# The last output pair and the next stage's first chunks of a ten-stage transformer kernel, worked off in two halves of the tokens

## Chip, cores and metric

One core of a Trainium2 chip. The metric is the device time of one execution in microseconds, lower is better; times are medians of several executions.

## What is computed

Three transformer layers over 512 tokens of width 1024, in float32. The first has a mixer of dilated attention, a state-space scan and a gated recurrence, then a SwiGLU feed-forward; the two that follow have a feed-forward, a mixer (block-sparse attention with compressed keys beside a retention), an attention over 256 memory tokens and a second feed-forward. Around every stage stands a root-mean-square norm:

```python
def rms_norm(x, g):
    xf = x.astype(jnp.float32)
    y = xf * lax.rsqrt(jnp.mean(xf * xf, axis=-1, keepdims=True) + EPS)
    return (y * g.astype(jnp.float32)).astype(x.dtype)
...
x = x + 0.5 * rms_norm(swiglu(rms_norm(x, pre_g), ...), post_g)
```

The mixer and the memory attention have the factor 1 in place of 0.5. Where two stages meet, the output y of one needs its own norm before it is added to x, and the new x needs another one before it is the input of the next.

## The kernel before, in words

**Layout.** x lies in SBUF with the features on the 128 partitions and 512 tokens along the columns, as 8 tiles of 128x512. Each float32 product is three matmuls (`mm3`, lines 255 to 257): operands are kept as a high part (rounded to the matmul's format) and a low part, and high x high, low x high and high x low are added in PSUM. Weights come as chunks of 8 tiles x 256 columns, in two DMAs of 512 KB (halves) on SyncE's queue. ScalarE makes the high part of a half (`weight_hi`, line 235), GpSimd the low part (`weight_lo`, line 249). Four slots hold halves; a slot is free when the chunk two before has been used.

**Engines.** Each engine has a program written out by hand, stage after stage, and works in that order; semaphores tie them. TensorE's order is the one given here.

**The end of a stage** (`OutProj`, `OutSums`). The output has 8 tiles in four pairs. A pair is 22 (feed-forward) or 8 (mixer, attention) tiles deep, in chunks of at most 8; each chunk runs its first output tile over all depths, then its second (`pe_stationary`). After a pair, ScalarE copies the tile out of PSUM (line 508) and squares it (line 511), VectorE adds the squares (line 497). Sums over the partitions are matmuls against a column of 1/1024 (`pe_token_means`, line 355): those of the first seven tiles run before the last product, those of the eighth after it. In the first block's feed-forward (`onto`) VectorE adds the product to x first (line 491).

**Between stages** (`Entry`). The means get epsilon on VectorE (line 542), the power -1/2 on GpSimd (line 547), and TensorE spreads the roots over the partitions (line 555) into a row bank; `pe_keep_busy` (line 562) stands before and after. VectorE meanwhile makes the low parts of the second chunk's weights. Then, tile by tile: y times gain and root (line 609; with kind "final" x itself, line 612, and no add), x plus y (line 619), the high part of x times the next gain on ScalarE (line 672), the low part on VectorE (line 624). VectorE issues them in the order scale of the next tile, low, add of the next tile. The input is not divided by its own root; results of the first products are multiplied with that row later. ScalarE squares the new x (line 661), four tiles beside the high parts, four after them; VectorE adds the squares (line 648) after its last tile.

**The start of a stage** (`pe_by_tile`, line 317 on). The first two chunks run together, tile by tile, as soon as a tile's low part is there. Then `pe_then` (line 716 on) waits for the last sum of squares, makes the means of x (line 355), and goes on with the third chunk; the row of roots follows after a few products.

**Start and end.** At the start ScalarE squares x (line 377), GpSimd adds the squares (line 389), TensorE sums them (line 346), and GpSimd makes the power (line 417) behind four low parts of weights; x comes in four DMAs, the constants (1.1 MB) between the first and the second. At the end (`Exit`) VectorE scales and adds (lines 746 and 750) and one DMA stores 2 MB. In the retention VectorE sums and centres each head's output (lines 2549 and 2555), ScalarE squares it with an accumulator (line 2519).

## Time and profile before

| what | value |
|---|---|
| time, median of 3 (lowest, highest) | 3376.74 us (3374.31, 3379.72) |
| the profiled execution's own time | 3378.53 us |
| its span, first to last instruction | 3377.2 us |
| mean granted TensorE clock | 0.987 |
| TensorE busy | 97% |
| VectorE, ScalarE, GpSimd busy | 38%, 36%, 39% |
| DMA, mean over the span | 85 GB/s |

Busy shares are means over the span. TensorE's busy time counts a matmul from its issue to its modelled end, so that overlapping ones hide short gaps; the spacing of their starts tells more. PEclk is the share of full speed (2.4 GHz) that was granted: 1.0, or 0.5 (1.2 GHz). A row of the timeline has start, duration, engine, line, operation, output<-inputs, count, and in brackets the idle time before it with what ended it. PE is TensorE, PEld its weight loads, DVE VectorE, ACT ScalarE, POOL GpSimd, SP SyncE. A plain float32 matmul (lines 346, 355, 555) appears as two instructions, so 4 of them are counted as x8.

### The profile page before, as it was taken

The numbers are of one execution on the slowest core, as the hardware profiler recorded it, in microseconds if no ns is written. First come the engines' busy times: TensorE is split into PE (matmuls) and PEld (weight loads), VectorE is DVE, ScalarE is ACT, GpSimd is POOL, SyncE is SP. The second block draws the span as 40 slices with busy tenths as digits, with TensorE's granted clock in tenths as the row PEclk, the third lists the DMA queues.
The fourth block names the chain that finished last, engine by engine and source line by source line (L and its number), as shares of the span: only waits on it lengthen the run. The fifth ranks groups of instructions, "written<-read, shape, count | busy, mean of one in ns | idle before, by whom it ended". The sixth has DMA issues, their size and how long they took to land.

```text
span 3377.2 us, 42103 instructions
## 1 busy us (share of the span) xinstructions
PE 3261.2 (97%) x16304; PEld 2676.1 (79%) x16304; DVE 1299.0 (38%) x2343; ACT 1219.4 (36%) x2237; POOL 1307.8 (39%) x831
## 2 busy tenths in 40 slices
PE   5999999999999999999999999999999999999997
PEld 4886788887888788887678887888787887678886
DVE  4564343205330434644263304431144563353311
ACT  4454332223222344553332223322344554332221
POOL 3452344443444343343234443444342243234442
PEclk9998999999999999999999999999999999999999
DMA  3221132232322232122122232332241122123231
GB/s 127 77 74 50 57 101 93 95 105 75 100 97 95 81 128 63 51 82 81 50 81 94 97 103 75 100 100 94 94 138 51 44 83 75 50 75 106 94 101 61
DMA packets 79109, 287.08 MB, mean 85 GB/s; under 512 B 8896, under 2 KB 9152, under 8 KB 78400
## 3 DMA queue, kind: packets, MB, share of 16 engines
q1 hardware_dynamic: 77616, 278.42, 25.1%
q10 hardware_dynamic: 1296, 5.98, 0.5%
q8 instruction: 131, 2.15, 0.3%
q14 instruction: 66, 0.54, 0.0%
HBM read 282.26 MB, written 2.10 MB: 84 GB/s over the span
## 4 chain that ended last, share of the span: by engine, by line
PE 83%; DVE 6%; POOL 3%; ACT 3%; issue 3%; DMA 1%; ACTq 0%; POOLq 0%; DVEq 0%
PE bank L255 25%; PE bank L257 24%; PE bank L256 24%; PE bank L965 3%; POOL wlo L249 2%; PE bank L941 2%; PE bank L952 2%; DVE hlo L624 1%; ACT hhi L672 1%; DVE x L619 1%; ACT whi L235 1%; PE bank L2684 1%; PE bank L555 1%; DVE m_xbc L1558 1%; POOL stat L547 1%
## 5 line engine op out<-in xcount | busy, mean ns | idle before, releaser
L249 POOL TENSOR_TENSOR wlo<-raw,whi 128x1024 fp32r<-128x1024 f32 (+2 forms) x782 | 1260.7, 1627 | 1881.0 <-ACT whi L235 1846.8
L255 PE MATMUL bank<-hhi,whi 128*128 128x512 f32 x2416 | 964.7, 399 | 19.0 <-POOL wlo L249 10.8
L256 PE MATMUL bank<-hlo,whi 128*128 128x512 f32 x2456 | 958.6, 390 | 0.0
L257 PE MATMUL bank<-hhi,wlo 128*128 128x512 f32 x2416 | 944.2, 391 | 0.0
L235 ACT ACTIVATE whi<-raw 128x1024 fp32r<-128x1024 f32 (+1 forms) x536 | 534.8, 1034 | 384.7 <-PE bank L257 374.1
L255 PEld LDWEIGHTS bank<-hhi,whi 128*128 128x128 f32 x2416 | 455.4, 188 | 125.0 <-issue 30.0
L256 PEld LDWEIGHTS bank<-hlo,whi 128*128 128x128 f32 x2456 | 463.3, 189 | 91.3 <-issue 1.2
L257 PEld LDWEIGHTS bank<-hhi,wlo 128*128 128x128 f32 x2416 | 454.8, 188 | 96.9
L255 PE MATMUL bank<-ff_ahi,whi 128*128 128x512 f32 x880 | 342.8, 390 | 0.0
L257 PE MATMUL bank<-ff_ahi,wlo 128*128 128x512 f32 x880 | 342.4, 389 | 0.0
L256 PE MATMUL bank<-ff_alo,whi 128*128 128x512 f32 x840 | 326.8, 389 | 0.0
L497 DVE TENSOR_TENSOR tmp<-tmp,tmp 128x512 f32<-128x512 f32 x60 | 48.0, 800 | 562.3 <-ACT tmp L511 562.3
L850 ACT ACTIVATE ff_ahi<-tmp 128x512 fp32r<-128x512 f32 x110 | 69.6, 633 | 444.6 <-DVE tmp L873 444.6
L863 DVE TENSOR_TENSOR tmp<-bank,row 128x512 f32<-128x512 f32 x110 | 75.0, 690 | 366.5 <-PE bank L257 319.0
L980 ACT ACTIVATE att_s<-att_s,stat 128x32 f32<-128x32 f32 (+4 forms) x224 | 110.0, 491 | 275.5 <-DVE stat L1012 274.5
L257 PEld LDWEIGHTS bank<-ff_ahi,wlo 128*128 128x128 f32 x880 | 165.2, 188 | 34.3
L255 PEld LDWEIGHTS bank<-ff_ahi,whi 128*128 128x128 f32 x880 | 165.2, 188 | 34.1
L256 PEld LDWEIGHTS bank<-ff_alo,whi 128*128 128x128 f32 x840 | 157.7, 188 | 32.7
L844 ACT ACTIVATE tmp<-tmp 128x512 f32<-128x512 f32 x110 | 68.7, 630 | 308.4 <-DVE tmp L863 308.4
L871 DVE TENSOR_TENSOR tmp<-bank,row 128x512 f32<-128x512 f32 x110 | 75.8, 689 | 223.9 <-PE bank L257 223.9
L255 PE MATMUL bank<-whi,hhi 128*128 128x256 f32 x448 | 134.5, 300 | 0.1
L1008 DVE SCALAR_TENSOR_TENSOR att_s<-consts,bank 128x32 f32<-128x32 f32 (+4 forms) x192 | 72.9, 380 | 158.1 <-PE bank L941 157.7
(343 smaller groups left out, 4165.8 us busy)
## 6 DMA issues: line engine op xcount, KB each, us to landing
raw<-wstream SPq DMA_DIRECT2D x516, 512.0 KB, 3.7
raw<-wstream SPq DMA_DIRECT2D x20, 256.0 KB, 3.0
x<-xT ACTq DMA_DIRECT2D x4, 512.0 KB, 12.9
xa_v<-memT ACTq DMA_DIRECT2D x2, 1024.0 KB, 4.7
outT<-x SPq DMA_DIRECT2D x1, 2048.0 KB, 6.2
consts<-consts ACTq DMA_DIRECT2D x1, 1135.0 KB, 9.5
m_lw<-lru_w ACTq DMA_DIRECT2D x1, 544.0 KB, 3.5
par<-par SPq DMA_DIRECT2D x2, 248.0 KB, 14.1
```

What stands on the lines that cost most here:

```text
L235: a.activation(h.hi[:, 0:h.cols], h.raw[:, 0:h.cols], ACT.Copy).then_inc(h.hi_made.sem)
L249: last = g.tensor_tensor(h.lo[:, o:o + step], h.raw[:, o:o + step], h.hi[:, o:o + step].bitcast(F32), ALU.subtract)
L255: t.matmul(out, l[0], r[0], start=start, stop=False)
L256: t.matmul(out, l[0], r[1], start=False, stop=False)
L257: return t.matmul(out, l[1], r[0], start=False, stop=stop)
L844: a.activation(k.tmp[2 + m][:, :], k.tmp[m][:, :], ACT.Tanh, scale=0.5).then_inc(self.tanh.sem)
L850: a.activation(self.ahi[:, o:o + T], k.tmp[m][:, :], ACT.Copy).then_inc(self.hi_made.sem)
L863: v.tensor_tensor(k.tmp[m][:, :], k.bank[gate.banks[m]][:, :], k.row[:, :], ALU.mult).then_inc(self.normed.sem)
L871: v.tensor_tensor(k.tmp[m][:, :], k.bank[up.banks[m]][:, :], k.row[:, :], ALU.mult).then_inc(self.up.sem)
L965: last = t.matmul(k.bank[b][:, at:at + DH], p[0:rows, kb * P:(kb + 1) * P], u["v"](kb), start=kb == 0, stop=kb == nb - 1, skip_group_check ...
L980: a.activation(s[:, 0:n], s[:, 0:n], ACT.Exp, bias=k.stat[:, 80 + step % 4:81 + step % 4], accum_out=self.sums(g)[0][:, step % group:step ...
L1008: v.scalar_tensor_tensor(s[:, 0:n], u["dist"], u["slope"], k.bank[b][:, 0:n], ALU.mult, ALU.add).then_inc(self.biased.sem)
```

## The change

Eight boundaries and the exit go by halves of 256 tokens. A stage's last pair keeps half 0 of both output tiles in one bank and half 1 in the other: its earlier chunks run both halves product by product (`pe_both`), the last chunk all of half 0 and then all of half 1 (`pe_halves`), with half 0's sums, roots and row placed between half 1's products. Squares and copies of the two tiles are one ScalarE instruction a half. The input is made in 16 half tiles, half 0 first, and the next stage's first two chunks run once a half (`pe_by_tile_halves`); half 1's sums and row stand after tiles 0 and 2 of half 0. So each of these products is two matmuls of 256 columns, with the weights loaded twice. The second chunk's first half of weights lies in memory of the stage that ends (`spare`), and GpSimd makes its low part; the other half's low part moves from VectorE to GpSimd, in four pieces. `pe_keep_busy` goes. The boundary from the first mixer to its feed-forward stays as it was, as a class of its own. Further: at the start TensorE sums the squares tile by tile, the low part of the fourth half comes after the power, and most of the constants load last; the exit scales by halves and stores in four DMAs; the retention takes its sums from ScalarE's accumulator, centres within the square and the gating, and gates with one instruction a chunk.

```diff
+def mm3_half(k, out, l, r, half, opens):
+    t, r = k.nc.tensor, [x[:, half * TH:(half + 1) * TH] for x in r]
+    t.matmul(out, l[0], r[0], start=opens, stop=True, skip_group_check=True)
+    t.matmul(out, l[0], r[1], start=False, stop=True, skip_group_check=True)
+    return t.matmul(out, l[1], r[0], start=False, stop=True, skip_group_check=True)
...
+def pe_by_tile_halves(k, chunks, part, ready, then):
+    t = k.nc.tensor
+    for half in range(2):
+        for i in range(KT + len(chunks) - 1):
+            for lag, ch in enumerate(chunks):
+                kk = i - lag
+                if not 0 <= kk < KT:
+                    continue
+                if half == 0:
+                    pe_half_begin(k, ch, kk)
+                if lag == 0:
+                    for mark in ready(kk, half):
+                        t.wait_ge(*mark)
+                for m, b in enumerate(ch.banks):
+                    if half == 0 and kk == 0 and ch.free[m] is not None:
+                        t.wait_ge(*ch.free[m])
+                    last = mm3_half(k, k.bank[b][:, half * TH:(half + 1) * TH], ch.weights(kk, m * P, P), part(kk), half,
+                                    half == 0 and kk == 0)
+                    if half == 1:
+                        pe_step_end(ch, last, kk, kk == KT - 1, m == len(ch.banks) - 1)
+            then(half, i)
...
-        t.wait_ge(*self.added[-1])
-        if self.free is not None:
-            t.wait_ge(*self.free)
-        pe_token_sums(self.k, self.k.tmp[2][:, :], 0, True).then_inc(self.sums.sem)
+        for n in range(KT):
+            t.wait_ge(*self.sq[n])
+            pe_token_sums(self.k, self.tile(n)[:, :], 0, n == 0).then_inc(self.summed.sem)
...
+    def act_squares(self, half):
+        a, k = self.k.nc.scalar, self.k
+        a.wait_ge(*self.added[2 + half])
+        a.wait_ge(*(self.kept[6 + half] if self.onto else self.last.done[half]))
+        src = self.half_of(k.x, half) if self.onto else self.both(self.in_bank(half))
+        a.activation(self.both(self.squares(half)), src, ACT.Square).then_inc(self.sq.sem)
+    def act_keep(self, half):
+        a, k = self.k.nc.scalar, self.k
+        if not self.onto:
+            a.activation(self.half_of(self.y, half), self.both(self.in_bank(half)), ACT.Copy).then_inc(self.kept.sem)
...
+    def pe_six(self, half):
+        t = self.k.nc.tensor
+        if half == 0:
+            t.wait_ge(*self.added[-1])
+            if self.free is not None:
+                t.wait_ge(*self.free)
+        else:
+            t.wait_ge(*self.roots[0].mean[0])
+        self.pe_add(self.k.tmp[2], half * TH, half, half == 0)
+    def pe_two(self, half):
+        self.k.nc.tensor.wait_ge(*self.sq[6 + half])
+        self.pe_add(self.squares(half), 0, half, False)
+        self.pe_add(self.squares(half), TH, half, False).then_inc(self.mean.sem)
...
+        k.elsewhere[self.first + 1] = stage.spare()
...
+        self.before = sums.roots = [HalfRoot(k, sums, half, (row_bank, sums.b)[half]) for half in range(2)]
...
     def dve(self):
         k, v = self.k, self.k.nc.vector
-        if self.kind == "plain":
-            for n in range(KT):
-                self.low(n)
-        else:
-            self.before.dve()
-            weight_lo(k, self.first + 1, e=v)
-            v.wait_ge(*self.before.rows[0])
-            self.scale(0)
-            self.add(0)
+        self.before[0].dve()
+        for half in range(2):
+            v.wait_ge(*self.before[half].rows[0])
+            self.scale(0, half)
+            self.add(0, half)
             for n in range(KT):
                 if n + 1 < KT:
-                    self.scale(n + 1)
-                self.low(n)
+                    self.scale(n + 1, half)
+                self.low(n, half)
                 if n + 1 < KT:
-                    self.add(n + 1)
-            acc = k.tmp[2]
-            for n in range(1, KT):
-                v.wait_ge(*self.sq[n])
-                if n >= 2:
-                    v.wait_ge(*self.sq_added[n - 2])
-                v.tensor_tensor(acc[:, :], acc[:, :], self.sq_tile(n)[:, :], ALU.add).then_inc(self.sq_added.sem)
+                    self.add(n + 1, half)
+                if half == 0 and n == 0:
+                    self.sums.dve_half(1)
+                if half == 0 and n == 1:
+                    self.before[1].dve()
+        acc = k.tmp[2]
+        for n in range(1, KT):
+            v.wait_ge(*self.sq[n])
+            if n >= 2:
+                v.wait_ge(*self.sq_added[n - 2])
+            v.tensor_tensor(acc[:, :], acc[:, :], self.sq_tile(n)[:, :], ALU.add).then_inc(self.sq_added.sem)
...
     def act(self):
         k, a = self.k, self.k.nc.scalar
-        for n in range(KT):
-            if self.kind == "plain":
-                a.wait_ge(*self.sums.kept[n])
-                if n == 0:
-                    a.wait_ge(*self.cat_read)
-            else:
-                a.wait_ge(*self.added[n])
-            a.activation(k.hhi[:, self.tile(n)], k.x[:, self.tile(n)], ACT.Copy, scale=self.gain_in(n)).then_inc(self.hi_made.sem)
-            if self.kind != "plain" and n < 4:
-                self.square(n)
+        for half in range(2):
+            for n in range(KT):
+                o = self.tile(n, half)
+                a.wait_ge(*self.added[KT * half + n])
+                a.activation(k.hhi[:, o], k.x[:, o], ACT.Copy, scale=self.gain_in(n)).then_inc(self.hi_made.sem)
+                if half == 0 and n == 0:
+                    self.sums.act_squares(1)
+                if half == 0 and n == 1:
+                    weight_hi(k, self.first + 1, 1)
+                if half == 0 and n == 2:
+                    self.sums.act_keep(1)
+                if half == 1 and n < 4:
+                    self.square(n)
         weight_hi(k, self.first + 2, 0)
-        if self.kind != "plain":
-            for n in range(4, KT):
-                self.square(n)
+        for n in range(4, KT):
+            self.square(n)
         weight_hi(k, self.first + 2, 1)
...
     def pool(self):
-        if self.before is not None:
-            self.before.pool()
-        else:
-            weight_lo(self.k, self.first + 1)
-        weight_lo(self.k, self.first + 2, 0)
+        for half in range(2):
+            self.before[half].pool()
+        weight_lo(self.k, self.first + 1, 1, pieces=4)
+        weight_lo(self.k, self.first + 2, 0, pieces=4)
         self.root.pool()
...
+    def pe_first(self, chunks, part):
+        def then(half, i):
+            if (half, i) == (0, 0):
+                self.sums.pe_two(1)
+            if (half, i) == (0, 2):
+                self.before[1].pe()
+        pe_by_tile_halves(self.k, chunks, part, lambda n, half: [self.lo_made[KT * half + n]], then)
+    def pe_then(self, steps):
         t, k = self.k.nc.tensor, self.k
-        if self.kind == "plain":
-            return
         t.wait_ge(*self.sq_added[-1])
         if self.free is not None:
             t.wait_ge(*self.free)
         pe_token_means(k, k.tmp[2], self.sums.b, True, True).then_inc(self.mean.sem)
...
+            v.wait_ge(*self.before[half].rows[0])
+            for n in range(KT + 1):
+                if n < KT:
+                    o = slice(n * T + half * TH, n * T + (half + 1) * TH)
+                    y = sums.y[:, o]
+                    if n == KT - 2:
+                        v.wait_ge(*sums.kept[6 + half])
+                    v.scalar_tensor_tensor(y, y, self.gain(n), self.before[half].row(), ALU.mult, ALU.mult).then_inc(self.scaled.sem)
+                if n > 0:
+                    o = slice((n - 1) * T + half * TH, (n - 1) * T + (half + 1) * TH)
+                    v.wait_ge(*self.scaled[KT * half + n - 1])
+                    v.scalar_tensor_tensor(k.x[:, o], sums.y[:, o], self.factor, k.x[:, o], ALU.mult, ALU.add).then_inc(self.added.sem)
+                if half == 0 and n == 2:
+                    self.before[1].dve()
...
+    def pe_both(self, k0, nk, ch):
+        self.pe_open(ch)
+        for m in range(2):
+            for kk in range(nk):
+                if m == 0:
+                    pe_half_begin(self.k, ch, kk)
+                for half in range(2):
+                    last = self.product(ch, kk, k0, m, half)
+                pe_step_end(ch, last, kk, kk == nk - 1, m == 1)
...
+    def pe_halves(self, k0, nk, ch):
+        sums = self.sums
+        self.pe_open(ch)
+        for m in range(2):
+            for kk in range(nk):
+                if m == 0:
+                    pe_half_begin(self.k, ch, kk)
+                if m == 1 and kk == nk - 1:
+                    sums.pe_six(0)
+                last = self.product(ch, kk, k0, m, 0)
+        last.then_inc(ch.done.sem)
+        n = 0
+        for k1 in range(0, nk, 4):
+            for m in range(2):
+                for kk in range(k1, min(k1 + 4, nk)):
+                    if n == 3:
+                        sums.pe_two(0)
+                    if n == 9:
+                        sums.roots[0].pe()
+                    if n == 10:
+                        sums.pe_six(1)
+                    last = self.product(ch, kk, k0, m, 1)
+                    n += 1
+                    if m == 1 and kk == nk - 1:
+                        last.then_inc(ch.done.sem)
+                    elif m == 1 and kk == 3:
+                        last.then_inc(ch.early.sem)
...
+            if pair == 3 and last and self.by_half:
+                weight_hi(self.k, ch.c + 2, 0)
+                self.sums.act_squares(0)
+                self.sums.act_keep(0)
+                continue
...
+        if self.by_half:
+            weight_lo(self.k, self.chunks[-1][4].c + 2, 0)
...
+    def spare(self):
+        put = self.k.arena(self.k.at_big, self.k.big_end)
+        return put("ff_spare_hi", HALF, F32R), put("ff_spare_lo", HALF, F32R), self.down.chunks[-3][4].done[-1]
...
-                a.wait_ge(*self.centred[c])
+                a.wait_ge(*self.summed[c])
                 for hh in range(4):
                     n = 4 * c + hh
                     if n >= 2:
                         a.wait_ge(*self.sq[n - 2])
-                    a.activation(self.dump(hh), self.columns(m.qr, hh, c), ACT.Square, accum_out=k.stat[:, 16 + n:17 + n]).then_inc(self.sq.sem)
+                    a.activation(self.dump(hh), self.columns(m.qr, hh, c), ACT.Square, bias=k.stat[:, n:n + 1],
+                                 accum_out=k.stat[:, 16 + n:17 + n]).then_inc(self.sq.sem)
...
-                v.tensor_reduce(total, m.qr[:, :].rearrange("p (h t) -> p h t", h=4)[:, :, c * P:(c + 1) * P], AX_X, ALU.add).then_inc(self.summed.sem)
-                v.wait_ge(*self.summed[2 * c])
                 v.tensor_scalar(total, total, -1.0 / 128, None, ALU.mult).then_inc(self.summed.sem)
-                v.wait_ge(*self.summed[2 * c + 1])
-                for hh in range(4):
-                    o = self.columns(m.qr, hh, c)
-                    last = v.tensor_scalar(o, o, total[:, hh:hh + 1], None, ALU.add)
-                last.then_inc(self.centred.sem)
...
-        if n == 1:
-            a.dma_start(k.consts[:, :], k.dram["c"]).then_inc(m.const_there.sem, 16)
-            a.dma_start(k.par1[:, :], k.dram["p1"]).then_inc(m.const_there.sem, 16)
         o = slice(n * 2 * T, (n + 1) * 2 * T)
         a.dma_start(k.x[:, o], k.dram["x"][:, o]).then_inc(m.x_there[n].sem, 16)
-    m.sq0.act()
+        if n == 0:
+            a.dma_start(k.consts[:, 0:early], k.dram["c"][:, 0:early]).then_inc(m.const_there.sem, 16)
+            a.dma_start(k.par1[:, :], k.dram["p1"]).then_inc(m.const_there.sem, 16)
+    a.dma_start(k.consts[:, early:], k.dram["c"][:, early:]).then_inc(m.later_there.sem, 16)
+    for n in range(KT):
+        m.sq0.act_tile(n)
+        if n % 2:
+            weight_hi(k, n // 4, n // 2 % 2)
...
-    m.sq0.pool()
     weight_lo(k, 0)
-    weight_lo(k, 1)
-    for s in m.stages:
+    weight_lo(k, 1, 0)
+    for n, s in enumerate(m.stages):
         if not isinstance(s, ToH):
             s.pool()
+        if n == 0:
+            weight_lo(k, 1, 1)
...
-    s.wait_ge(*m.out.added[-1])
-    s.dma_start(k.dram["out"], k.x[:, :]).then_inc(m.stored.sem, 16)
-    s.wait_ge(*m.stored[0])
+    for n in range(4):
+        half, o = n // 2, n % 2 * 4 * T
+        part = lambda x: x[:, o:o + 4 * T].rearrange("p (n t) -> p n t", n=4)[:, :, half * TH:(half + 1) * TH]
+        s.wait_ge(*m.out.added[4 * n + 3])
+        s.dma_start(part(k.dram["out"]), part(k.x)).then_inc(m.stored.sem, 16)
+    s.wait_ge(*m.stored[3])
```

## Rows read from the trace of the kernel before

**Rows 1.** The page's part on the chain that ended last, by engine.

```profile
PE 83%; DVE 6%; POOL 3%; ACT 3%; issue 3%; DMA 1%; ACTq 0%; POOLq 0%; DVEq 0%
```

**Rows 2.** Windows: start:end, length, busy us (count) by engine, PEclk, DMA share, GB/s.

```profile
850.00:935.00 85.00, 85.00 (x376) 70.41 (x375) 31.36 (x40) 25.29 (x32) 38.35 (x16) 1.00 0.29 95
1134.05:1144.07 10.02, 8.99 (x25) 5.00 (x25) 5.63 (x8) 4.21 (x6) 1.93 (x1) 0.66 0.31 105
1144.07:1166.55 22.48, 22.15 (x97) 18.02 (x97) 19.92 (x27) 11.07 (x16) 2.61 (x1) 1.00 0.07 24
1135.40:1142.10 6.70, 6.36 (x17) 3.91 (x18) 3.79 (x5) 1.83 (x2) 1.93 (x1) 0.50 0.37 120
```

**Rows 3.** Timeline from one stage's last matmul to the next input: start, us, engine, line.

```profile
1134.90 1.52 PE L355 MATMUL bank<-consts,tmp 128*128 128x1 f32 x8 [0.69 <-ACT tmp L511]
...
1136.70 1.93 POOL L547 TENSOR_TENSOR stat<-stat,consts 128x4 f32<-128x4 f32 x1 [7.93 <-DVE stat L542]
...
1140.80 0.75 DVE L609 SCALAR_TENSOR_TENSOR ff_y<-ff_y,par,bank 128x512 f32<-128x512 f32 x1 [1.71 <-PE bank L555]
```

**Rows 4.** Timeline of the same boundary, around the sums of the new x.

```profile
1158.75 7.47 DVE L648 TENSOR_TENSOR tmp<-tmp,tmp 128x512 f32<-128x512 f32 x7
...
1159.07 2.61 POOL L249 TENSOR_TENSOR wlo<-raw,whi 128x1024 fp32r<-128x1024 f32 x1 [20.45 <-ACT whi L235]
...
1171.28 0.47 PE L255 MATMUL bank<-hhi,whi 128*128 128x512 f32 x1 [0.90 <-POOL wlo L249]
```

**Rows 5.** Groups by line, 1140 to 1167: count | busy us, mean ns | idle before.

```profile
L624 DVE SCALAR_TENSOR_TENSOR hlo<-x,par,hhi 128x512 fp32r<-128x512 f32 x8 | 6.0, 751 | 1.7 <-ACT hhi L672 0.8
L672 ACT ACTIVATE hhi<-x,par 128x512 fp32r<-128x512 f32 x8 | 5.8, 724 | 12.9 <-DVE x L619 12.9
L619 DVE SCALAR_TENSOR_TENSOR x<-ff_y,x 128x512 f32<-128x512 f32 x8 | 5.5, 684 | 0.0
```

**Rows 6.** Single lines at 256 columns: ns min/median/max, first and last start, form.

```profile
L2373 DVE SCALAR_TENSOR_TENSOR xa_mlo<-xa_v,par,xa_mhi x16: 473/485/687, 1393.0 to 2703.3; 128x256 fp32r<-128x256 f32 x16
...
L2262 ACT ACTIVATE xa_mhi<-xa_v,par x16: 492/498/504, 1392.5 to 2699.0; 128x256 fp32r<-128x256 f32 x16
```

**Rows 7.** PE's timeline, first and last of 20 matmuls over 256 columns.

```profile
91.97 0.28 PE L255 MATMUL bank<-whi,hhi 128*128 128x256 f32 x1
...
94.25 0.28 PE L256 MATMUL bank<-wlo,hhi 128*128 128x256 f32 x1
```

**Rows 8.** Pieces of the chain and PE's timeline at the second layer's first boundary.

```profile
2433.38 1.07 PE bank L355 x8
...
2463.64 0.95 PE L355 MATMUL bank<-consts,tmp 128*128 128x1 f32 x8
```

**Rows 9.** Timeline of the start, up to the first product.

```profile
16.43 1.15 ACT L377 ACTIVATE tmp<-x 128x512 f32<-128x512 f32 x2 [0.67 <-DMA x<-xT]
...
23.58 9.78 POOL L249 TENSOR_TENSOR wlo<-raw,whi 128x1024 fp32r<-128x1024 f32 x4
23.76 1.84 PE L346 MATMUL bank<-consts,tmp 128*128 128x1 f32 x8 [23.76 <-POOL tmp L389]
...
33.33 1.01 POOL L417 TENSOR_TENSOR stat<-stat,consts 128x4 f32<-128x4 f32 x1
...
38.79 0.77 PE L255 MATMUL bank<-hhi,whi 128*128 128x512 f32 x1 [2.32 <-DVE hlo L453]
```

**Rows 10.** Timeline of the end of the kernel.

```profile
3356.04 0.40 PE L257 MATMUL bank<-ff_ahi,wlo 128*128 128x512 f32 x1
...
3360.71 1.41 DVE L746 SCALAR_TENSOR_TENSOR ff_y<-ff_y,par,bank 128x512 f32<-128x512 f32 x2 [2.34 <-PE bank L555]
```

**Rows 11.** DMA issues by size: count, KB each, median us to landing.

```profile
raw<-wstream SPq DMA_DIRECT2D x516, 512.0 KB, 3.7
```

**Rows 12.** Groups by line in the retention: count | busy us, mean ns | idle.

```profile
L2555 DVE TENSOR_SCALAR m_qr<-m_qr,stat 128x128 f32<-128x128 f32 x32 | 13.0, 467 | 0.3
...
L2519 ACT ACTIVATION_READ_ACCUMULATOR tmp<-m_qr 128x1 f32 x32 | 6.0, 186 | 0.0
```

More of the change, by code:

```diff
@@ L15 @@
 TB = T // P
+TH = T // 2
 D = 1024
@@ L191, in __init__, with stands_in @@
         self.released = None
+        self.free = self.before.released if self.before is not None else None
+    def stands_in(self, hi, lo, free):
+        self.hi, self.lo, self.free = hi, lo, free
 class Chunk:
@@ L789, in dve @@
         for pair, k0, nk, last, ch in self.chunks:
-            if last:
+            if pair == 3 and last and self.by_half:
+                self.sums.dve_half(0)
+            elif last:
                 for m, b in enumerate(ch.banks):
```

339 lines of the change are left out of this document (230 added, 109 removed).

## The prediction, made before the changed kernel ran

> **What bounds the kernel now.** I read the page first, then the windows, then the timeline of one boundary between stages, then the groups and single lines that price its parts. TensorE carries the chain for 83% of the span [rows 1]; where a stage runs, 376 matmuls over 512 columns start in 85 us, 0.226 us each, at the full granted clock [rows 2]. What can be won lies where the stages meet. From the last product at 1134.05 to the first of the next stage 10.0 us pass at a mean granted clock of 0.66, and the next stage's first two chunks, 96 matmuls worth 21.7 us, take 22.5 [rows 2]. The 10 us are a chain: squares, sums on TensorE at 1134.90, the power on GpSimd (1.93 us), the roots' rows, and VectorE's first scaling at 1140.80 [rows 3]. But a second chain runs behind it: VectorE makes the eight input tiles, then adds the squares of the new x, 7 adds in 7.47 us from 1158.75 to 1166.22 [rows 4], and the means of x open the third chunk at 1166.55 [rows 2]. VectorE and TensorE get there together, with 0.3 us between them. So an earlier first product is worth something only if the squares of x come earlier too. There are eight such boundaries and the exit.
>
> **The parts.** I count each boundary from s, the start of the output pair's last chunk. After a feed-forward that chunk has 36 matmuls: 36 x 0.226 + 0.8 for the token sums = 8.95, so s = 1125.1 and the means of x come at s + 41.45.
>
> *Half matmuls.* 20 matmuls over 256 columns start within 2.28 us, 0.120 each [rows 7], so a split matmul costs 0.240 for 0.226, 13.5 ns more. The pair's two earlier chunks (96 matmuls, after a feed-forward alone) cost 1.3 us, the next stage's first two chunks another 1.3, the last chunk 0.5. The Trainium skill (TensorE: Matmul & The Clock Gate, Back-to-back issue gap) gives N / 2.4 + 2.5 ns at the full clock, so 2.5 ns for a split instead of 13.5, some 0.25 us instead of 1.3 for each 96; the row decides.
>
> *Half 0's chain* goes under half 1's products. Half 0 ends at s + 4.7 (36 x 0.120 + 0.4); square 0.2 + 0.6; the sums stand behind three products (to 6.6), then 0.16 and the power, about 1.0 now that VectorE no longer makes the weights' low part beside it. TensorE has its ninth product behind it at 8.75, after which it makes the rows. VectorE's first scaling starts at s + 9.35, against 15.7 (1140.80) now: 6.35 earlier.
>
> *The input by halves.* At 512 columns an add takes 0.68, the high part 0.72 on ScalarE, the low part 0.75 [rows 5]; they hang in a ring (add, high, low, next add), and the eight tiles run at 2.14 us apiece. At 256 columns the low part takes 0.485 and the high part 0.50 [rows 6], the add 0.68 - 0.27 = 0.41. With 0.04 for each signal the ring is 0.41 + 0.04 + 0.50 + 0.04 + 0.40 = 1.39 us a half tile. Sixteen of them are 22.3 us where 17.1 stood: 5.1 us given back. TensorE would take 12 x 0.120 = 1.44 a half tile, so the first products wait for nothing.
>
> *Moved work.* ScalarE's high part of the second chunk's second half (1.05), its squares and copy of half 1, now stand in that ring: 0.3. GpSimd takes that half's low part from VectorE, in four pieces, beside the ring. In the trace an add that meets GpSimd's weight instruction waits for its end: the 7 adds hold 2 us more than 7 x 0.8 [rows 4]; four quarter pieces of 0.65 cost the ring about 1.0. So the adds start at 9.35 + 1.5 (first low) + 22.3 + 0.3 + 1.0 - 0.7 (the last low starts, not ends, a ring) = s + 33.75, where they start now at s + 33.65. They meet four pieces instead of one long instruction: 6.9 us. The means of x come at s + 40.65, with the earlier chunks 41.95. TensorE reaches them at 36.3: it then stands idle for 4.4 us.
>
> *After mixer and attention* the last chunk has 48 matmuls: now 10.85 + 0.8 = 11.65 to its end, 44.15 to the means. New: half 0 ends at 6.2, and half 1's sums, 0.8 later, hold up VectorE: 43.2.
>
> *Two kinds now.* The power takes 1.93 in four of the eight boundaries and 1.0 in four; the latter reach the means in 30.3 us from the first L355 row (2433.38 to 2463.64) [rows 8] where 1134.90 to 1166.55 is 31.65: 1.4 less. The change: two feed-forward boundaries of the long kind +0.5 each, one of the short +1.9; one long after a mixer -1.0, three short +0.4. Together +3.1.
>
> *The boundary with no add* (the final norm of the first block): its ring is 0.4 shorter, so VectorE leads, and TensorE's 192 half matmuls end at s + 36.4; with 1.3, 37.7 against 41.45: -3.8.
>
> *The clock.* Now it falls inside the gaps, where TensorE has little to do (0.50 from 1135.4 to 1142.1) [rows 2]. The new idle of 4.4 us precedes full work. After the means now stand 2.7 us of products, then a wait for the third chunk's low part, 4.7 us behind the means (1171.28) [rows 4]; that leaves 1.2 us of cover. Half clock for some microseconds costs between 0 and 2.3; I take 0.5 at seven boundaries: +3.5.
>
> *The start.* Now squares are added on GpSimd, four weight instructions follow (9.78), then the power at 33.33, and the first product 5.46 after it [rows 9]. New: TensorE sums eight tiles, 1.6 to 1.8 each at that clock (1.84 for one from rest) [rows 9], from about 6 to 20; x lands with 1.1 MB of constants behind instead of before it, by 15 to 18; GpSimd has three weight instructions before the power, free by 17 to 20. Power at 19.5, product at 25.0 against 38.79: -13.8, between -11 and -16.5.
>
> *The exit.* From the last product (3356.04 + 0.23) to VectorE's first scaling at 3360.71 stand 4.4 us, so it comes at s + 13.4, and 16.5 us later the span ends [rows 10]. New: first scaling at 9.35 + 1.3 = 10.65; 32 halves at 0.37 (two now start 0.64 apart, 0.27 less for half the columns) = 11.8, 1.0 waiting for half 1, and 3.7 for a last DMA of 512 KB [rows 11]: 16.5 as well. With three transfers ahead of the last one I take -2.5.
>
> *The retention.* VectorE loses 13.0 us of centring and some reductions and gains a multiplication a chunk; ScalarE gains as many accumulator reads as there are now, 6.0 us [rows 12]. TensorE's projections cover both; uncovered, +3 or -5. I take -1.
>
> **The sum:** 3.1 - 3.8 + 3.5 - 13.8 - 2.5 - 1 = -14.5. Against the profiled execution's own 3378.5 that is 3364; the median of the three runs stands 1.8 lower, so 3362.3, rounded to 3363.
>
> **The rivals.** *A, the squares don't hold.* If VectorE and GpSimd don't collide (pieces fall where VectorE reads one tile only), the means come at s + 38.2 (40.8 after a mixer), 2.4 earlier at seven boundaries, and the idle is too short for the clock to fall: -17 - 3.5 more, 3342. Against it speak the adds of [rows 4]. 20%.
> *B, slower.* The ring on VectorE is longer than 1.39: by 0.1 us, from collisions and signals (L2373's own maximum is 0.687 against 0.485) [rows 6], it puts the means 1.6 later, and TensorE, idle 6 us, comes back to 2.3 us of half-clock loss: 7 x (1.6 + 1.8) = 24 more, 3386. It decides from a ring of 1.45. The Trainium skill (SBUF — State Buffer, two separate sides) calls the port pair of VectorE and GpSimd an exclusive lock for a whole instruction, which speaks for this one; the trace agrees [rows 4]. 17%.
> *C, the start gives little.* x or the weights land as late as now and the sums queue: -5 instead of -13.8: 3371. 13%.
> *D, it doesn't hide.* TensorE works in order, and a sum or row that comes late holds the products behind it: 1 us at each boundary, 3371 too. 8%.
> Forecast 42%.
>
> **How the numbers follow.** A measurement here can tell about 0.2%, 6.7 us. Faster: all of A, nearly all of the forecast (37 of 42), a third of the rest. Slower: B and a little of the doubtful. That makes 0.60, 0.21, 0.19. The range runs from A's value to short of B's, 3342 to 3381; the forecast's own is 3354 to 3373.
>
> **What would show it.** First product near 25. In the boundary windows: no gap over 1 us before the first products, 256-column matmuls 0.120 apart, but an idle of some 4 us before L355's successor (the means of x) in seven places, with half clock around it, and VectorE's tiles 1.39 us apart. No such idle is A; a ring over 1.45 and half clock in the third chunk is B; a first product after 32 is C. The prediction is wrong if the squares of x are not what TensorE waits for.

## The result, and the profile after

The changed kernel took 3390.68 us (median of 6 runs, 3385.75 to 3393.40), the kernel before 3376.56 beside it: ratio 1.0041, 95% interval 1.0031 to 1.0051. It is slower by 14 us, where I had 14 us faster. The profiled execution spans 3391.7 us.

The page's chain by engine (before: [rows 1]), and the windows of the same boundary (columns as in [rows 2]): the last chunk of the output pair, the stretch to the next stage's first product, the first two chunks, the stretch to the means of x, and the stretch at half clock.

```profile
PE 85%; DVE 8%; ACT 4%; issue 2%; POOL 1%; DMA 1%; ACTq 0%; DVEq 0%; POOLq 0%
```
```profile
1112.09:1122.94 10.85, 10.85 (x94) 10.80 (x92) 1.44 (x4) 3.44 (x5) 6.41 (x4) 1.00 0.44 146
1122.94:1123.88 0.94, 0.16 (x3) 0.03 (x1) 0.75 (x4) 0.76 (x2) 0.00 (x0) 1.00 0.00 0
1123.88:1149.04 25.16, 25.03 (x204) 24.47 (x204) 21.24 (x48) 13.32 (x24) 6.28 (x8) 1.00 0.07 22
1149.04:1153.19 4.15, 0.01 (x1) 0.00 (x0) 3.68 (x5) 2.21 (x3) 1.96 (x2) 0.88 0.24 72
1152.20:1159.00 6.80, 5.81 (x18) 4.94 (x19) 3.33 (x4) 0.00 (x0) 3.35 (x2) 0.50 0.21 72
```

The 10 us between the stages [rows 2] are down to 0.9. In their place TensorE stands idle for 4.15 us later on, and comes back at half clock. The timeline and the list of TensorE's waits say for what:

```profile
1126.56 3.42 POOL L257 TENSOR_TENSOR wlo<-raw,whi 128x256 fp32r<-128x256 f32 x4
...
1146.25 6.88 DVE L862 TENSOR_TENSOR tmp<-tmp,tmp 128x512 f32<-128x512 f32 x7
...
1146.85 4.16 POOL L257 TENSOR_TENSOR wlo<-raw,whi 128x256 fp32r<-128x256 f32 x4 [16.87 <-ACT whi L243]
...
1153.19 1.87 PE L396 MATMUL bank<-consts,tmp 128*128 128x1 f32 x8 [4.15 <-DVE tmp L862]
```
```profile
PE bank L396 <- DVE tmp L862: 29.4, 7, 4.5
...
PE bank L263 <- DVE xa_mlo L2674: 5.0, 2, 2.5
```

These are seven waits for the adds of squares, 29.4 us in all, and two in the mixers of 2.51 us each, which were 0.67 each before. The start came 10.1 us earlier, 3.7 less than forecast:

```profile
9.54 13.82 PE L387 MATMUL bank<-consts,tmp 128*128 128x1 f32 x64 [9.54 <-DMA par<-par]
24.80 2.08 PE L451 MATMUL bank<-consts,stat 128*128 128x128 f32 x8 [1.44 <-POOL stat L443]
29.26 0.77 PE L263 MATMUL bank<-hhi,whi 128*128 128x512 f32 x1 [2.38 <-DVE hlo L479]
```

**Where the time went.** The start of the means of x, the same work in both traces, gives the distance (after minus before) as the program goes on: -10.1 after the first stages, -14.2 at the boundary of the final kind, -13.4 (1153.19 against 1166.55), -6.1 (1573.42 against 1579.47), -1.6, +1.4, +5.0, +14.5 (2891.43 against 2876.91), +17.1 (3031.86 against 3014.80); at the last high part of a weight +18.3; at the end +14.5. So the start gave 10.1, the final kind 4.0, the exit 3.8, and from there to there seven boundaries and two mixers took 32.4, where my terms for them (3.1 + 3.5 - 1) made 5.6.

### The profile page after: what moved, and what is told of

It is laid out like the page before. It is cut to its first block, busy times and chain, and to the rows that moved or that the text cites. A ratio compares the mean times of both kernels' runs of the same rounds, so it can differ in the third digit from the quotient of the medians.

```text
span 3391.7 us, 45793 instructions
## 1 busy us (share of the span) xinstructions
PE 3281.8 (97%) x17988; PEld 2783.1 (82%) x17988; DVE 1297.6 (38%) x2495; ACT 1242.9 (37%) x2333; POOL 1357.5 (40%) x897
## 4 chain that ended last, share of the span: by engine, by line
PE 85%; DVE 8%; ACT 4%; issue 2%; POOL 1%; DMA 1%; ACTq 0%; DVEq 0%; POOLq 0%
PE bank L263 23%; PE bank L265 22%; PE bank L264 22%; PE bank L1260 3%; PE bank L271 2%; PE bank L273 2%; PE bank L272 2%; PE bank L1236 2%; PE bank L1247 2%; ACT hhi L883 2%; DVE hlo L838 2%; DVE tmp L862 1%; POOL wlo L257 1%; DVE x L833 1%; PE bank L2993 1%
## 5 line engine op out<-in xcount | busy, mean ns | idle before, releaser
L257 POOL TENSOR_TENSOR wlo<-raw,whi 128x256 fp32r<-128x256 f32 (+2 forms) x838 | 1301.1, 1569 | 1880.7 <-ACT whi L243 1838.3
L263 PE MATMUL bank<-hhi,whi 128*128 128x512 f32 x2160 | 868.4, 402 | 10.1 <-POOL wlo L257 3.0
L264 PE MATMUL bank<-hlo,whi 128*128 128x512 f32 x2190 | 860.1, 393 | 0.0
L265 PE MATMUL bank<-hhi,wlo 128*128 128x512 f32 x2160 | 849.1, 393 | 0.0
L263 PEld LDWEIGHTS bank<-hhi,whi 128*128 128x128 f32 x2160 | 410.8, 190 | 96.9 <-issue 15.1
L264 PEld LDWEIGHTS bank<-hlo,whi 128*128 128x128 f32 x2190 | 416.6, 190 | 82.8 <-issue 1.0
L265 PEld LDWEIGHTS bank<-hhi,wlo 128*128 128x128 f32 x2160 | 409.9, 190 | 87.9
L263 PE MATMUL bank<-ff_ahi,whi 128*128 128x512 f32 x660 | 256.7, 389 | 0.0
L265 PE MATMUL bank<-ff_ahi,wlo 128*128 128x512 f32 x660 | 256.7, 389 | 0.0
L264 PE MATMUL bank<-ff_alo,whi 128*128 128x512 f32 x630 | 245.1, 389 | 0.0
```

The source lines that it names most:

```text
L257: last = g.tensor_tensor(h.lo[:, o:o + step], h.raw[:, o:o + step], h.hi[:, o:o + step].bitcast(F32), ALU.subtract)
L263: t.matmul(out, l[0], r[0], start=start, stop=False)
L264: t.matmul(out, l[0], r[1], start=False, stop=False)
L265: return t.matmul(out, l[1], r[0], start=False, stop=stop)
```

## The experiments

Medians, and the difference from the kernel before in the same session (the changed kernel: +14.1). Differences between two runs are taken from that column. A product is three matmuls (`mm3`). From e3 on the recorded texts often name one product too few: by the edits the means of x stand after the 5th product of the third chunk in e5, after the 7th in e7 to e9, and after the 9th in e3, e11, e13 and e14; the rows of the root follow four products later (five in e3).

| run | us | from before | ratio, 95% |
|---|---|---|---|
| e1 earlier Retention | 3386.33 | +8.0 | 1.0014 to 1.0033 |
| e2 nine idle matmuls | 3410.26 | +31.9 | 1.0081 to 1.0107 |
| e3 means after the 9th product | 3399.06 | +20.7 | 1.0053 to 1.0079 |
| e4 before + new Retention | 3384.20 | +5.8 | 1.0007 to 1.0024 |
| e5 means after the 5th | 3388.95 | +11.9 | 1.0020 to 1.0045 |
| e6 four idle matmuls | 3380.43 | +3.3 | 1.0002 to 1.0020 |
| e7 e5 and e1, earlier high part | 3388.64 | +11.6 | 1.0024 to 1.0049 |
| e8 e7, low parts whole | 3375.85 | -1.2 | 0.9991 to 1.0009 |
| e9 high parts ahead | 3357.82 | -19.8 | 0.9928 to 0.9955 |
| e10 before + new start | 3367.91 | -9.7 | 0.9956 to 0.9981 |
| e11 e9, one place earlier | 3343.40 | -34.5 | 0.9888 to 0.9918 |
| e12 e10 + e9's order | 3390.56 | +12.7 | 1.0025 to 1.0050 |
| e13 e12 + e11's order | 3370.88 | -6.7 | 0.9971 to 0.9988 |
| e14 e11, new Retention | 3354.16 | -23.4 | 0.9916 to 0.9943 |

**e1, e4: the retention alone.** e1 puts the class Retention of the kernel before ("the earlier Retention" from here on) into the changed kernel; e4 puts the new class into the kernel before.

> The changed kernel with the earlier Retention class put back (sums by a reduction on VectorE, centring in place, squares without a bias, gating in one pass of four after the root). Theory: the new gating's four operations run on VectorE while GpSimd takes a weight's low part (2.54 us each group, and 6.20 us for the GpSimd operations beside them), so the low parts of the next projections come late and TensorE stands 2.5 us in each mixer, followed by a stretch at half clock; with the old class back each mixer is 4 to 6 us shorter, some 8 to 12 us in all, and the two 2.5 us waits on the low part are gone: 3379 to 3383. Rival: the waits there come from the mixer's input, which arrives with another spacing after the change, and not from the retention; then the time stays within 3 us of the changed kernel, 3388 to 3393.

> The kernel before with only the new Retention class. Theory: the new gating is what costs about 5 us in each mixer, whatever the boundaries do: 3384 to 3388, slower than the kernel before by 7 to 12 us. Rival: it costs only where the changed boundaries have moved GpSimd's work under it; then within 3 us of before (my forecast had it 1 us faster).

The new class costs 6.1 us in the one and 5.8 in the other. VectorE and GpSimd in the changed kernel, then TensorE:

```profile
1387.81 6.20 POOL L257 TENSOR_TENSOR wlo<-raw,whi 128x256 fp32r<-128x256 f32 x8 [21.48 <-ACT whi L243]
...
1391.88 2.54 DVE L2850 SCALAR_TENSOR_TENSOR m_qr<-m_qr,stat,m_gr 128x128 f32<-128x128 f32 x4
1394.45 0.17 DVE L2854 TENSOR_SCALAR stat<-stat 128x4 f32<-128x4 f32 x1
1394.53 1.12 DVE L2870 TENSOR_SCALAR tmp<-bank,consts 128x128 f32<-128x128 f32 x4
1395.57 0.47 DVE L2674 SCALAR_TENSOR_TENSOR xa_mlo<-xa_v,par,xa_mhi 128x256 fp32r<-128x256 f32 x1
...
1396.10 0.39 PE L263 MATMUL bank<-xa_mhi,whi 128*128 128x256 f32 x1 [2.51 <-DVE xa_mlo L2674]
```

The four gating operations, 0.35 us each elsewhere (the median), take 2.54 together beside GpSimd's pieces, and the low part of the memory's input stands behind them. In e1 that wait is 0.7 us at both places. My bounds for the uncovered case were +3 and -5; it is the upper one, at each mixer. The gain of 8 to 12 that e1 expected, and the loss of 7 to 12 in e4, were too high (e4's time lies just inside its range).

**e2, e6: is it the idle time that halves the clock?** In front of the means of x:

```diff
+        for _ in range(9):     # e6: 4, and none at the final kind
+            pe_keep_busy(k, k.chunks[self.first + 2].banks[0], T)
         t.wait_ge(*self.sq_added[-1])
```

> The changed kernel with nine idle matmuls (float32, 512 columns, into the bank that the third chunk will open) between the second chunk and the means of x, at each of the seven boundaries. They take 9 x 0.43 = 3.9 us, and the wait there was 4.15 us. Theory: the half clock right after that wait (6.8 us, about 1.66 us lost between the means and the root's rows) comes because TensorE stood idle; with the engine kept busy it goes, and 7 x 1.66 = 11.6 us come back less up to 0.3 us each where the idle matmuls end late: 3379 to 3383. Rival: the half clock comes on its own schedule and only moves elsewhere, as at other places in the trace; then the time stays at 3388 to 3394.

> e2 again with four idle matmuls in place of nine, and none at the boundary of the final kind, where there was no wait. One of them took 0.857 us in e2 (7.7 us for nine), so nine overfilled each wait by 3.6 us; four take 3.43 us and leave 0.7 us idle. Theory: e2 came out 19.5 us slower than the changed kernel, which is 7.7 + 7 x (7.7 - 4.15 - 1.66) = 20.9 with the half clock's 1.66 us won back at each of seven boundaries; with nothing overfilled the whole 7 x 1.66 = 11.6 us show: 3379, between 3376 and 3383. Rival: no clock was won in e2 and its sum is an accident of other waits; then the time stays at 3388 to 3393.

e2's own arithmetic was wrong: I had one idle matmul at 0.43 us, it took 0.86. e6 mends that. Its windows (the idle matmuls; from the means to behind the rows) and its timeline, where the changed kernel has 4.15 us of idle time and then a clock of 0.50:

```profile
1150.51:1154.79 4.28, 3.60 (x10) 1.33 (x8) 3.81 (x5) 2.21 (x3) 2.09 (x2) 1.00 0.26 78
1154.79:1161.20 6.41, 5.50 (x31) 4.54 (x32) 2.50 (x2) 0.00 (x0) 3.35 (x2) 1.00 0.17 56
```
```profile
1154.79 1.05 PE L396 MATMUL bank<-consts,tmp 128*128 128x1 f32 x8 [0.69 <-DVE tmp L867]
...
1159.62 0.47 PE L263 MATMUL bank<-hhi,whi 128*128 128x512 f32 x1 [0.90 <-POOL wlo L257]
...
1160.39 0.38 PE L730 MATMUL bank<-consts,stat 128*128 128x128 f32 x2
```

Means to rows take 5.60 us instead of 7.16, and the kernel 10.8 less, as the theory had it, for matmuls whose results nobody reads. The adds and the means come no earlier. So at these seven places the idle time in front is what lowered the clock from 2.4 to 1.2 GHz; in e2 too the stretches there are gone (5.49 us from means to rows at all seven).

**e3, e5: take the means later.** The third chunk does not need them:

```diff
-        t.wait_ge(*self.sq_added[-1])
-        pe_token_means(...)
         for n, _ in enumerate(steps):
-            if n == 4:
+            if n == 8:          # e5: 4
+                t.wait_ge(*self.sq_added[-1])
+                pe_token_means(...)
+            if n == 13:         # e5: 8
                 self.root.pe()
```

GpSimd makes both low parts of that chunk before the root; ScalarE its second high part between two squares.

> The changed kernel with the means of x and the root's rows taken later: the third chunk starts at once, the means stand after its ninth product and the rows after its thirteenth; its second half's high and low parts are made before the root for that. Theory: the 4.15 us of idle time at each boundary is there because the seven adds of squares start only after the last half tile. The third chunk does not need them; what it then waits for is its own low part, which ends at 1151.0 beside 1153.2 for the adds, so the idle time falls from 4.15 to about 2.1 us, and if it falls enough for the clock to stay up 1.66 us more: 7 x 2.1 = 15 to 7 x 3.7 = 26 us less, 3365 to 3376. Rival: the wait only moves (the low part of the third chunk's second half, or the row that the third chunk's evacuation waits for, is late by as much): 3386 to 3392.

> As e3, but with the means of x after the fourth product of the third chunk and the rows of the root after the eighth (e3: ninth and thirteenth). In e3 the idle time before the third chunk fell to 2.08 us, but the rows came so late that GpSimd, which waits for the root in order, made the next chunk's low parts 2.8 us late. Theory: with the rows as early as in the changed kernel that second wait goes, and the 2.1 us stay won at each of the seven boundaries: 3390.7 - 7 x 2.1 = 3376, between 3372 and 3380; the half clock stays, since TensorE still stands 2.1 us. Rival: what e3 lost was due to the low parts that were moved ahead of the root (they also delay it), and the time stays above 3388.

Both theories fall: e3 is 6.6 us slower than the changed kernel, more than even its rival had, and e5 only 2.2 faster, as its rival had it. TensorE's timeline in e5:

```profile
1155.61 0.47 PE L263 MATMUL bank<-hhi,whi 128*128 128x512 f32 x1 [2.09 <-POOL wlo L257]
1159.73 0.47 PE L263 MATMUL bank<-hhi,whi 128*128 128x512 f32 x1 [1.13 <-POOL wlo L257]
```
```profile
806.26 0.77 PE L263 MATMUL bank<-hhi,whi 128*128 128x512 f32 x1 [2.57 <-POOL wlo L257]
```

With the adds out of the way GpSimd is late three times: 2.09 and 1.13 us for the third chunk's halves, and 2.57 in four feed-forwards for a chunk whose high part ScalarE makes only behind the row and the second pair's tanh. From the first product on, TensorE's idle times over 0.3 us sum to 79 us in e5 and in the changed kernel. The waits moved.

**e7, e8, e9, e11: the chain of the weights.** All are variants of the changed kernel, with the earlier Retention.

> The changed kernel with the earlier Retention class of e1, the means of x after the sixth product of the third chunk and the rows after the tenth, and the high part of the third chunk's first half made 1.3 us earlier (after the sixth tile of the second token half instead of after the last). Theory: e1's 4.4 us, 7 x 2.1 us as in e5, and up to 1.3 us less idle time before the third chunk at each boundary, 9 us: 3390.7 - 4.4 - 14.7 - 9 = 3363; where the idle time of under a microsecond also keeps the clock up, 11.6 us less, 3351. Range 3348 to 3366. Rival: GpSimd's pieces now lie on VectorE's last operations of the ring and stretch them, and the by-tile part ends as much later; then no better than e5 with e1, 3370 or above.

> e7 with the low parts of these halves in one piece of 1024 columns instead of four of 256. Theory: a whole low part takes about 2.4 us against 4.16 us in four pieces with VectorE's adds between them, so the third chunk's low part is there 1 to 2 us earlier and the idle time before it is nil; VectorE waits up to 2.4 us once, which nobody waits for: up to 7 us less than e7. Rival: VectorE's operations of the ring stand behind the piece, so that the last tiles' low parts come up to 2.4 us later and the by-tile part with them: 7 to 15 us more than e7.

e7 went its rival's way. e8 against e7 is the price of four pieces: 12.8 us, more than the 7 at most that I expected. With a whole low part TensorE waits 1.30 us for the ring at the last tile (0.68 in e7), but the wait of 2.25 us in e7 is 0.91:

```profile
1153.10 0.39 PE L271 MATMUL bank<-hhi,whi 128*128 128x256 f32 x1 [1.30 <-DVE hlo L838]
1160.61 0.47 PE L263 MATMUL bank<-hhi,whi 128*128 128x512 f32 x1 [0.91 <-POOL wlo L257]
```

e9 starts the high part after the ring again, and moves two others ahead (each is then left out at its old place):

```diff
+        weight_hi(k, self.first + 3)
         a.wait_ge(*self.root.rows[0])        # Entry.act, before the row's copy
...
             if p > 0:
                 weight_hi(k, gate.c + 2)
+            else:
+                weight_hi(k, gate.c + 4)     # FeedForward.act, before the copies to ahi
```

> e8 with the high part of the third chunk's first half back at its place behind the last tile, and two high parts moved ahead on ScalarE: the fourth chunk's before the copy of the root's row, the fifth chunk's (feed-forwards alone) before the copies of the first gated pair. Theory: in e8 what TensorE waits for after the third chunk is a chain row copy, high part, GpSimd's low part (waits of 0.91, 0.76 and, in four feed-forwards, 2.79 us), and the early high part made GpSimd's piece stand on the ring (1.30 us at the last tile). The fourth chunk's wait and the 2.79 us go, the 1.30 us at seven boundaries become 0.2: 3375.9 - 4 x 3.5 - 7 x 1.1 = 3354, between 3350 and 3366. Rival: the waits sit in VectorE's chain from the row to the gated pair (14.6 us in every kernel so far) and come back at the next chunk's evacuation: within 5 us of e8, 3371 to 3381.

It is 18.5 us faster than e8, within its range. What is left at each of the seven boundaries is a wait of 2.17 us behind one of 0.33. ScalarE, VectorE and GpSimd say why:

```profile
1147.00 0.63 ACT L879 ACTIVATE tmp<-x 128x512 f32<-128x512 f32 x1 [0.20 <-DVE tmp L866]
1149.85 0.63 ACT L879 ACTIVATE tmp<-x 128x512 f32<-128x512 f32 x1 [2.22 <-DVE tmp L866]
1150.39 1.05 ACT L247 ACTIVATE whi<-raw 128x1024 fp32r<-128x1024 f32 x1
...
1146.28 9.49 DVE L866 TENSOR_TENSOR tmp<-tmp,tmp 128x512 f32<-128x512 f32 x7
...
1146.87 2.40 POOL L261 TENSOR_TENSOR wlo<-raw,whi 128x1024 fp32r<-128x1024 f32 x1 [16.88 <-ACT whi L247]
```

The sixth square waits for an add that meets GpSimd's piece (that add takes 2.75 us), and the high part waits in line behind it. e11 swaps them, and takes the means after the ninth product, the rows after the thirteenth.

> e9 with the high part of the third chunk's second half after the fifth square instead of the sixth, and the means of x after the eighth product of the third chunk, the rows after the twelfth. Theory: in e9 the sixth square waits 2.2 us for an add of VectorE that stands beside GpSimd's piece, and the high part behind it, so the second half's low part is 2.17 us late at each of the seven boundaries; one place earlier it is up to 1.4 us earlier: 3357.8 - 7 x 1.4 = 3348, between 3344 and 3354. Rival: the adds now end later (they stand beside the second piece too) and the means wait for them instead, or the row comes late for the next evacuation: 3356 to 3362.

It took 3343.4 us, 0.6 below its range. At the boundary TensorE's timeline holds one short wait:

```profile
1148.30 0.47 PE L267 MATMUL bank<-hhi,whi 128*128 128x512 f32 x1 [0.35 <-POOL wlo L261]
...
1154.76 1.05 PE L400 MATMUL bank<-consts,tmp 128*128 128x1 f32 x8
```

**e10, e12, e13: are the halves worth it?** e10 is the kernel before with the changed start; e12 adds e9's order on ScalarE and GpSimd, without halves; e13 also takes the means later, as e11.

> The kernel before with the changed start alone (squares of x summed on TensorE, constants in two parts, weights' high parts between the squares). Theory: the start gives what the drift between the two traces shows at the first stage, 10.2 us, and nothing gives it back: 3367 (from 3377), between 3365 and 3369. Rival: part of it is given back within the first mixer, as the first stages wait for the later constants or weights: 3370 or above.

> e10 (the kernel before with the changed start) with e9's reorderings and without the token halves: both low parts of the third chunk ahead of the root on GpSimd, the high parts of the fourth and fifth chunks ahead on ScalarE. It tells what the halves themselves are worth beside e9. Theory: without the halves the third chunk follows the tiles with no wait, so only the 0.9 us wait for the second half's low part goes, at eight boundaries: 3367.9 - 7 = 3361, between 3358 and 3365; e9's 3357.8, less its exit's 2.5, is then no better, and the halves gain nothing even where their waits are mended. Rival: the moved low part delays the root and the row, and the adds stand behind it: 3366 to 3372.

> e12 with the means of x after the eighth product of the third chunk, the rows after the twelfth, and the high part of the third chunk's second half after the fifth square, as in e11: e11 without token halves and without the changed exit. In e12 the third chunk waited 2.30 us for the adds at each boundary and ran at half clock after it. Theory: that wait is all that e12 lost, and without it only the 0.9 us per boundary of e10 are won: 3367.9 - 7 = 3361, between 3356 and 3366; against e11's 3343.4 the halves are worth some 15 us, of 17.6 less 2.5 for the exit, about 2 us at each boundary. Rival: the same order gives without halves what it gives with them, 3346 to 3350, and the halves are worth nothing.

The start is worth 9.7 us, as expected. e12 lost 22 us against e10, outside its theory and its rival: with two low parts under VectorE's adds the means come late there too, eight times (18.4 us in all, from the list of e12's waits):

```profile
PE bank L359 <- DVE tmp L637: 18.4, 8, 2.3
```

e13 takes that back but stays 3 us above e10, above its own range. In one and the same order the halves and the exit are worth 27.8 us (e13 to e11), some 24 without the exit's 3.8, 3 at each boundary. Against e10, the faster of the two kernels without halves, they are worth 24.8, some 21 without the exit. e12 alone would have overstated it: e9, of the same order on ScalarE and GpSimd, is 32.4 us faster.

**e14: the retention again, in e11.**

> e11 with the changed kernel's Retention class in place of the earlier one. Theory: its price is the mixer's own and does not hang on the boundaries: e1 and e4 gave 4.4 us and 5.8 us for both mixers together, so 3343.4 + 5 = 3348, between 3346 and 3351, with the wait for the low part at the first mixer at 2.5 us again. Rival: the mixer starts at another point against GpSimd's pieces here, and it costs nothing or gains 1 us: 3341 to 3344.

It costs 11.1 us, about twice as much as in e1 and e4, so theory and rival both miss it. The waits of 2.5 us are back in both mixers, each followed by a stretch at half clock, where e11 has none (windows of e11, then of e14, TensorE alone):

```profile
1390.00:1398.00 8.00, 8.00 (x64) 1.00 0.09 31
```
```profile
1390.00:1398.00 8.00, 7.18 (x35) 0.57 0.03 11
```

Two waits that are 1.85 us longer and two times 3.4 us lost to the clock make 10.5. In e1 and e4 some of that clock was lost in the mixers without the new class as well (a stretch of 3.4 us each at 1399 and 2710 in e1, at 2705 before).

## Why the prediction was wrong

**What held.** At the boundary the steps came out as worked: s = 1112.09; first scaling s + 9.53 (9.35), adds from s + 34.16 (33.75) in 6.88 us (6.9), means at s + 41.1 (40.65), idle 4.15 (4.4). The ring is 1.40 us (1.39), 33 half matmuls after s take 3.96, 0.120 each (the Trainium skill's formula for an isolated gap, TensorE: Matmul & The Clock Gate, Back-to-back issue gap, would make that 0.109; the trace decides again). The final kind gave 4.0 (3.8). From the forecast -14.5 to the +14.5 of the two profiled executions are 29.0 us, which the points below share out.

**What failed, first: the clock, "I take 0.5 at seven boundaries".** I knew that 4.4 us of idle time would precede full work, bounded the cost by 0 and 2.3, and took a value near the lower end, because a wait for the third chunk's low part "leaves 1.2 us of cover". Means to rows took 5.50 us at all seven before; now 7.15, 6.98, 7.47, 6.83, 6.00, 6.75 and 6.03, so 8.7 more where I had 3.5. All of these stretches at half clock end ahead of the rows. The cover was there, but smaller than 1.2: the 5.50 us hold the wait of 0.90 for the third chunk's low part [rows 4], which is gone in the changed kernel and back in e6. So the half clock cost 2.56 us at the first boundary (7.16 less 4.60 of work), and 0.90 of it was covered. Before, such stretches fell into the gaps between the stages, where they cost about 1 us, above all because the spread of the roots took 2.08 us, against 1.06 at full clock (the kernel before, line 555):

```profile
1138.68 2.08 PE L555 MATMUL bank<-consts,stat 128*128 128x128 f32 x8 [0.34 <-POOL stat L547]
```

Four more stretches of 3.4 us stand in the midst of stages of the changed kernel (from 1298.9, 1633.5, 2510.7 and 2616.5; the first and last of them as windows):

```profile
1298.90:1302.40 3.50, 3.50 (x19) 0.51 0.00 0
2616.50:2619.90 3.40, 3.40 (x19) 0.50 0.00 0
```

They cost 1.7 us each, 6.8 together, and the prediction had no term for them. Why they come is open: ahead of three of them TensorE's waits are the same in the kernel before, which runs there at full clock (0.62 and 0.59 us ahead of the first), and e13, without halves, has the first and the last as well (from 1307.2 and 2600.9). In e6 one of the four is left. Of the 8.7 us e6 won back 8.0 (5.60 at each boundary against 5.50).

**Second: the retention, "TensorE's projections cover both".** -1 was taken, +6 measured (e1, e4), so with 7 us this is the largest single term that was wrong. I had counted VectorE's time and not where it stands: the new gating lies beside GpSimd's low parts, and TensorE waits for what is queued behind it. My own row of an add held up by GpSimd [rows 4] said what happens there. The Trainium skill (SBUF — State Buffer, two separate sides) calls the port pair of the two engines an exclusive lock for a whole instruction, and e9's add of 2.75 us beside a piece of 2.40 agrees.

**Third: the start.** The sums start at 9.54, not "from about 6": TensorE waits for the parameters, which stand behind the first quarter of x and the early constants in ScalarE's queue. The sums' length (13.82, forecast 14) and the 5.5 us from the power to the first product were right. The start gave 10.1 instead of 13.8.

**Fourth, small:** the exit gave 3.8 instead of 2.5. Of the 32.4 us I can place 8.7 of clock behind the means and 6.8 in the midst of stages; 5.1 more of clock in the mixers (6.8 less the 1.7 that stood there before) and 3.7 of waits in them; and 1.3 for one wait on a high part (2.46 us at 2509, where the kernel before waits 1.18). The remaining 6.8 belong to the boundaries, where I had 3.1, and were not tested one by one. The 29.0 us are then 5.2 for the clock behind the means, 6.8 for it in the midst of stages, 9.8 in the mixers, 3.7 at the start, 1.3 for that wait and 3.7 at the boundaries, less 1.5 for the exit and the final kind.

**The rivals.** B had the right side and nearly the right size (3386), but by luck: the ring was 1.40 us, and the idle time not 6; its half clock came with 4.15. Its test, "it decides from a ring of 1.45", failed. The clock should have been a rival of its own. A is out (the adds hold 6.88 us), C and D too: the start gave 10.1, and TensorE's waits inside the last chunks are 0.8 at most. The chances were also added wrongly: the forecast's 37, A's 20 and a third of the rest make 0.64 or more for "faster", not 0.60.

**The point of the change was sound, its order was not.** The squares of x were what TensorE waits for in the kernel as changed, but I did not ask whether TensorE had to wait for them there. e11 keeps the halves, start and exit, takes the means nine products later, makes the low parts whole, moves three high parts ahead on ScalarE, and keeps the earlier Retention: 47 us less than the changed kernel, 34.5 less than the one before.

## What to carry to other kernels

When a gap is filled, look at what used to hide in it: here stretches at half clock, which cost about 1 us in the gap and 2.6 ahead of dense matmuls. Price a wait of several microseconds ahead of dense matmuls as the wait plus the clock behind it, and test the second part with a few idle matmuls. A wait removed from an in-order engine uncovers the next one in line (adds, then low parts, then the high part behind a square), so judge the idea only when the whole line has been moved; and put a control through the same reordering before saying what the idea is worth.

## What the runs showed of the hardware

Idle time of much the same length did not always bring the half clock, not even within one kernel. The 4.1 to 4.5 us ahead of the means brought it at all seven boundaries of the changed kernel, and the 2.5 us in the mixers at both places, there and in e14. The 2.30 us in e12 brought it at seven of eight places. The 2.1 us ahead of the third chunk brought it at one place of seven in e3 (1157.4), and in e5 at another one (1574.2) but not at the first; in e5 it came at four more only after the second wait, of 1.13. The 0.33 and 2.17 us in e9 brought it nowhere. Windows of e5, behind its first and its second wait of 2.09, TensorE alone:

```profile
1155.61:1159.61 4.00, 2.99 (x12) 1.00 0.41 134
1574.21:1577.61 3.40, 3.40 (x10) 0.50 0.44 154
```

What decides between them no run here shows, so such a term is a range and not a number.

A low part of 1024 columns takes GpSimd 2.40 us in one piece; in four with VectorE's adds between them 4.16, while the adds are lengthened only from 0.69 to 1.04. A whole piece holds a single add up to 2.75 us, and the seven adds take 7.47 us with one [rows 4] against 6.88, but it frees GpSimd sooner; that was worth 12.8 us between e7 and e8.
